# A two-layer decoder step on one core: window sums of the pooling tiles in two parts, other places for the sample's memory keys and values, and a new order of the last window groups

## The chip, the core and the metric

The kernel runs on one core of one Trainium2 chip. The metric is the device time of one launch in microseconds (us). Before the change the median of 3 runs is 1742.46 us (1741.4 to 1744.76). The profile was taken in a run of 1741.23 us, of which 1739.1 us lie between its first and its last instruction (the span).

TensorE multiplies matrices, VectorE (DVE) and ScalarE (ACT) read its results from PSUM, GpSimd (POOL) works in SBUF alone, and SyncE (SP) issues most transfers. Every engine takes its instructions in the order in which they are written; where one needs another's result, it waits on a semaphore.

## The reference, cut to what matters

One inference step: a prompt of 2048 tokens and a sample of 8 sequences of 8 tokens, width 1024, through a pooling layer (A) and a layer of sliding-window attention (B). Both share the branch that attends to 256 memory tokens with 4 heads.

```python
for i in range(N_A_LAYERS):                               # layer A
    z = rms_norm(x, norm_a[i]) @ w_in_a[i]
    u, gp, qm, gm = split(z)                              # 768, 768, 256, 256
    u_ext = concatenate([pool_prefix[i], u], axis=1)
    yp = pool_mixer(u_ext, pos, ...) * silu(gp)           # window means of 2, 4, 8, 16 rows, minus u, times mix_w
    ym = memory_branch(qm, gm, ..., mem_k[i], mem_v[i])   # softmax over 256 memory tokens
    x = x + concatenate([yp, ym]) @ w_out_a[i]
k, v = ...                                                # projected once after layer A
for j in range(N_B_LAYERS):                               # layer B
    q, gq, qm, gm = split(rms_norm(x, norm_b[j]) @ w_in_b[j])
    o = swa_banded(q, k, v, sinks)                        # prompt: blocks of 128 see themselves and the one before
    #   swa_window(q, k_all, v_all, ...)                  # sample: 128 cached keys and 8 new ones
    x = x + concatenate([o * silu(gq), memory_branch(...)]) @ w_out_b[j]
```

The prompt's memory keys and values are computed from `mem_prompt`. The sample's come from the caches `cache_mem_k` and `cache_mem_v`: per layer 8 sequences, each with 256 KB of keys and 256 KB of values in this layout.

## The kernel before

The prompt is cut into 8 tiles of 256 tokens. The program runs: a preparation (weights are scaled and split into two fp16 parts, a high and a low one), tile A0 with work of the preparation between its steps, seven more tiles of layer A, the sample in layer A (called SA), eight tiles of layer B, and the sample in layer B (SB). Every large product is three fp16 products (high x high, high x low, low x high), so a group of 256 output features for 256 tokens is 48 matmuls.

**A tile of layer A.** TensorE computes in order `qm` (memory queries), `u0` to `u2` (pooling inputs), the gates `g0` to `g2`, then `mix0` to `mix2` (the pooling products), `gm`, and four output groups `out0` to `out3`. Between them stand the memory branch's small products: transposed queries (L821), scores (L730), transposed weights (L738) and values (L748), and `largest` (L676), which spreads a maximum over all partitions for the scaling of layer B's weights; that scaling runs beside the tile on POOL (`gained`, L2300), DVE (`weight_top`, `scale_of`, `low_b`, L1621) and ACT (`high_half`, L1222). POOL normalises the queries (L2295), then waits until ACT has copied u2 and u1 (L1333), forms the running window sums of all six feature chunks together (L2374 to L2385), and normalises the softmax weights between them (`mem_norm`, L2306). DVE turns the sums into differences (L1798), and the `mix` matmuls (L768) wait for all six.

**A tile of layer B.** A window "group" is four heads of one block of 128 tokens, six groups a tile (0 to 5). Each goes round the engines: scores on TensorE (L1026), masks and maxima on DVE (`window_front`, L2094 to L2106), exponentials on ACT (L1445), sums on DVE (`window_back`), normalising on POOL (L2427), transposes on TensorE (L1034), masked weights on DVE (`window_weights`, L2124), values on TensorE (L1046), and gating on DVE (L2133). At the end of the tile the last groups alternate with pieces of the output groups (`split_out`, L778); a piece may start when DVE has split the gated features it reads (`gate_lows`, L1702).

**The sample.** Its memory keys and values come through `slot`: four places of 256 KB each. In SA the keys go through four places in `w_x` and the values through four in `x_buf`; in SB all sixteen pass through the same four places of `x_buf`. A place is loaded again when TensorE has counted up `slot_used` for the slot that it held (`load_slot`), and SP issues these loads in line with all its others. TensorE waits for each slot (`wait_slot`) in the scores (L933) and in the values (L954).

**PSUM.** `Ring` hands out banks in a fixed order: `Z` has two banks for the large products, `T` one for transposes and `largest`, `S` two for scores, `V` one for values. A writer waits until the bank's last reader is through.

```python
T = Ring(..., {"A": ["wt0", "qT", *PTM, "wt1", "ss"], ...})          # order in which T's bank is handed out
```

Of the kernel before, what the change touches and what calls it, by code (L numbers as in the profile page):

```python
# [14 lines left out]
P = 128  # L15
# [155 lines left out]
def build(nc, io):  # L171
    with ExitStack() as ctx:
# [173 lines left out]
        def slot(part, n):  # L346

            keys_a = part == "SA" and n < DB
            ring = w_x[:, 14 * P:14 * P + 2048] if keys_a else x_buf[:, 1 if part == "SA" else 0].rearrange("p k n -> p (k n)")
            return ring[:, (n % 4) * 512:(n % 4 + 1) * 512].rearrange("p (c n) -> p c n", c=2)  # L350

        def tile_of(d, t):
# [20 lines left out]
            "A": ["wt0", "qT", *PTM, "wt1", "ss"],  # L373
# [69 lines left out]
        win_sums = Signal(sem("win_sums"), {"A0": 1, "A": 1, "SA": 1})  # L443
        d_in = Signal(sem("d_in"), {"A0": 1, "A": 1, "SA": 1})
# [41 lines left out]
        def _(sp):  # L486
# [49 lines left out]
            def tile_a(t, p):  # L536
# [30 lines left out]
            for n in (*range(4, DB), *range(DB + 4, 2 * DB)):  # L567
# [28 lines left out]
            dma(io["swa_v_p"], v[:, 3]).then_inc(outputs, 16)  # L596
# [1999 lines left out]
```

## Time and profile before

| stretch | span, us | TensorE busy, us | granted clock |
|---|---|---|---|
| a tile A (344.0 to 425.0) | 81.0 | 77.04 | 1.00 |
| sample in layer A (748.5 to 812.6) | 64.1 | 40.08 | 0.76 |
| a tile B (1022.6 to 1126.7) | 104.1 | 99.40 | 1.00 |
| sample in layer B (1647.5 to 1739.1) | 91.6 | 63.99 | 0.75 |
| whole span | 1739.1 | 1574.5 | 0.967 |

The profiled execution took 1741.23 us, 2.13 us more than its span. A granted clock of 1.00 is 2.4 GHz, the higher of TensorE's two levels; a mean below 1 mixes it with 1.2 GHz. Matmuls overlap in the pipeline, so a busy TensorE isn't one at its peak, and the idle time in front of an instruction says more. In the timeline such idle time stands in brackets with what ended it; rows with "x48" merge that many instructions, from the start of the first to the end of the last.

### The profile page before, as it was taken

How to read it: one execution, taken by the hardware profiler on the slowest of the kernel's cores; microseconds unless marked ns; L12 is line 12 of the kernel's file. 1: busy time of each engine (PE TensorE's matmuls, PEld its weight loads, DVE VectorE, ACT ScalarE, POOL GpSimd, SP SyncE). 2: the span in 40 equal slices, each digit the busy share in tenths (PEclk: the TensorE clock that was granted, in tenths of full speed). 3: DMA queues.
4: the chain of work that ended last, by engine and by line, in shares of the span. 5: the costliest groups of instructions: out<-in, count | busy, mean ns of one | idle time of the engine just before them, and what ended most of it. 6: DMA issues, size and time to landing. Idle time of an engine off the chain costs nothing.

```text
span 1739.1 us, 31207 instructions
## 1 busy us (share of the span) xinstructions
PE 1574.5 (91%) x13448; PEld 1230.9 (71%) x13448; DVE 933.3 (54%) x1842; ACT 509.9 (29%) x1227; POOL 501.3 (29%) x353
## 2 busy tenths in 40 slices
PE   5787999999999999967999999999999999999976
PEld 2466888878788888855675767757586675767745
DVE  6876463545455454534563836547374563836531
ACT  2542222232323231311332514224142331514220
POOL 2631325242424142221322213132121322213120
PEclk9989999999999999987999999999999999999986
DMA  9021212122121213178101010000101001010031
GB/s 400 33 79 49 98 49 98 70 77 98 49 98 49 107 41 118 42 245 318 59 1 49 1 49 1 19 31 1 49 1 50 1 2 49 2 49 1 29 129 49
DMA packets 27400, 119.12 MB, mean 68 GB/s; under 512 B 3488, under 2 KB 3936, under 8 KB 16480
## 3 DMA queue, kind: packets, MB, share of 16 engines
q1 hardware_dynamic: 25184, 108.33, 16.7%
q10 hardware_dynamic: 2080, 8.80, 1.3%
q8 instruction: 107, 1.75, 0.4%
q14 instruction: 29, 0.24, 0.0%
HBM read 81.38 MB, written 37.64 MB: 68 GB/s over the span
## 4 chain that ended last, share of the span: by engine, by line
PE 74%; DVE 14%; ACT 5%; POOL 4%; issue 2%; DMA 1%; ACTq 0%; DVEq 0%; SPq 0%; POOLq 0%
PE ps_z L665 21%; PE ps_z L778 18%; PE ps_z L654 15%; PE ps_z L768 3%; PE ps_s L1026 2%; PE ps_z L836 2%; PE ps_t L738 2%; PE ps_p L748 2%; POOL tiny_sb L2271 2%; PE ps_p L1046 1%; DVE w_x_sb L1621 1%; DVE ph_sb L2124 1%; PE ps_z L978 1%; POOL pm_sb L2295 1%; ACT pm_sb L1258 1%
## 5 line engine op out<-in xcount | busy, mean ns | idle before, releaser
L665 PE MATMUL ps_z<-xn_sb,w_in_sb 128*128 128x256 f16 (+1 forms) x4752 | 506.6, 266 | 3.5 <-DVE gate_sb L1676 2.5
L665 PEld LDWEIGHTS ps_z<-xn_sb,w_in_sb 128*128 128x128 f16 x4752 | 429.3, 99 | 61.6 <-issue 7.1
L778 PE MATMUL ps_z<-pm_sb,w_out_sb 128*128 128x256 f16 x2048 | 348.8, 273 | 3.3 <-DVE x_buf_sb L1742 3.3
L778 PE MATMUL ps_z<-gate_sb,w_out_sb 128*128 128x256 f16 x1024 | 279.9, 273 | 0.0
L2271 POOL TENSOR_TENSOR tiny_sb<-tiny_sb 128x2 f32<-128x2 f32 (+4 forms) x56 | 94.2, 1682 | 535.7 <-DVE tiny_sb L1643 300.8
L778 PEld LDWEIGHTS ps_z<-pm_sb,w_out_sb 128*128 128x128 f16 x2048 | 202.3, 99 | 29.3 <-DVE x_buf_sb L1742 4.1
L654 PE MATMUL ps_z<-w_in_sb,xn_sb 128*128 128x512 f16 (+2 forms) x840 | 181.7, 376 | 0.0
L1634 DVE TENSOR_REDUCE tiny_sb<-scr_sb 128x8 f32<-128x512 f32 (+3 forms) x64 | 38.0, 593 | 237.4 <-ACT scr_sb L1202 157.5
L654 PEld LDWEIGHTS ps_z<-w_in_sb,xn_sb 128*128 128x128 f16 (+1 forms) x840 | 83.0, 99 | 94.1 <-issue 0.2
L1202 ACT ACTIVATE scr_sb<-ps_z,tiny_sb 128x256 f32<-128x256 f32 (+2 forms) x94 | 42.6, 489 | 346.0 <-PE ps_z L654 270.1
L778 PEld LDWEIGHTS ps_z<-gate_sb,w_out_sb 128*128 128x128 f16 x1024 | 100.5, 98 | 11.5
L1742 DVE SCALAR_TENSOR_TENSOR x_buf_sb<-ps_z,tiny_sb,x_buf_sb 128x512 f32<-128x512 f32 x64 | 48.0, 749 | 109.5 <-PE ps_z L778 109.4
L2427 POOL TENSOR_TENSOR ph_sb<-ph_sb,tiny_sb 128x512 f32<-128x512 f32 x48 | 50.0, 1042 | 193.2 <-DVE tiny_sb L2116 193.2
L1445 ACT ACTIVATE ph_sb<-ph_sb,tiny_sb 128x128 f32<-128x128 f32 x192 | 74.5, 390 | 101.5 <-DVE tiny_sb L2106 101.5
L654 PE MATMUL ps_z<-w_x_sb,xn_sb 128*128 128x512 f16 (+1 forms) x408 | 91.2, 384 | 2.3 <-issue 2.3
L2276 POOL TENSOR_TENSOR big_sb<-big_sb 128x1024 f32<-128x1024 f32 x17 | 40.0, 2354 | 170.3 <-ACT big_sb L1194 170.3
L2306 POOL TENSOR_TENSOR pm_sb<-pm_sb,tiny_sb 128x1024 f32<-128x1024 f32 x32 | 62.3, 1958 | 79.9 <-DVE tiny_sb L1669 79.9
L1216 ACT ACTIVATE xn_sb<-big_sb 128x2048 f16<-128x2048 f32 x18 | 34.4, 1911 | 167.0 <-DVE big_sb L1565 167.0
L1676 DVE SCALAR_TENSOR_TENSOR gate_sb<-scr_sb,ps_z 128x512 f32<-128x512 f32 (+1 forms) x72 | 45.9, 638 | 69.4 <-ACT scr_sb L1247 68.7
L654 PEld LDWEIGHTS ps_z<-w_x_sb,xn_sb 128*128 128x128 f16 (+1 forms) x408 | 40.5, 100 | 49.7 <-issue 4.9
L1258 ACT ACTIVATE pm_sb<-ps_s,tiny_sb 128x256 f32<-128x256 f32 x128 | 58.6, 475 | 57.6 <-DVE tiny_sb L1664 57.6
L1247 ACT ACTIVATE scr_sb<-ps_z,tiny_sb 128x512 f32<-128x512 f32 (+1 forms) x72 | 46.8, 650 | 81.9 <-PE ps_z L665 81.9
(267 smaller groups left out, 2377.8 us busy)
## 6 DMA issues: line engine op xcount, KB each, us to landing
x_buf_sb<-x SPq DMA_DIRECT2D x18, 1024.0 KB, 4.8
w_x_sb<-w_b SPq DMA_DIRECT2D x14, 1024.0 KB, 4.7
x<-x_buf_sb SPq DMA_DIRECT2D x9, 1024.0 KB, 4.0
y<-x_buf_sb SPq DMA_DIRECT2D x9, 1024.0 KB, 3.9
w_in_sb<-w_in_a SPq DMA_DIRECT2D x8, 1024.0 KB, 25.5
w_in_sb<-parts ACTq DMA_DIRECT2D x8, 1024.0 KB, 10.6
parts<-ph_sb SPq DMA_DIRECT2D x14, 512.0 KB, 3.0
parts<-w_x_sb SPq DMA_DIRECT2D x14, 512.0 KB, 3.0
```

The source lines that it names most:

```text
L654: last = mm(out, xs[:, x, kc, tok:tok + n], w[:, gs[0]:gs[-1] + 1, ws, kc, :], start=(kc == 0 and ws + x == 0), stop=(kc == KC - 1 and ws ...
L665: last = mm(ps_z[:, b, half * NT:half * NT + n], w_split[:, g, ws, kc, half * P:(half + 1) * P], xs[:, x, kc, 0:n], start=(kc == 0 and ws ...
L768: last = mm(out, mix_w[:, blocks.index((o, i)), :], src, start=(i == ins[0]), stop=(i == ins[-1]))
L778: last = mm(ps_z[:, b, half * NT:(half + 1) * NT], w_out_split[:, g, ws, kc, half * P:(half + 1) * P], gate_parts[x][:, kc, 0:NT], start=( ...
L1247: f(pair[0], pair[1], ACT.Tanh, scale=halfunit).then_inc(scr_in.sem, 1)
L1258: last = f(pm[:, blk, e, :], ps_s[:, b, e // 2, (e % 2) * NMEM:(e % 2 + 1) * NMEM], ACT.Exp, bias=m_neg[:, blk, e:e + 1], scale=SCALE, acc ...
L1445: f(sw[:, n % 2, e, :], sw[:, n % 2, e, :], ACT.Exp, bias=w_neg[:, n % 2, e:e + 1], scale=SCALE, accum_out=w_sum[:, n % 2, e:e + 1])
L1676: ve.scalar_tensor_tensor(gate[:, c:c + 2, 0:n], pair[0], 1.0, pair[1], ALU.add, ALU.mult)\
L1742: ve.scalar_tensor_tensor(x, ps_z[:, b].rearrange("p (c n) -> p c n", c=2)[:, :, 0:n], unit, x, ALU.mult, ALU.add).then_inc(Z.free[b], 1)
L2271: return tt(out, x, power[0:n, 0:w], ALU.pow)
L2306: tt(pm[:, blk], pm[:, blk], r, ALU.mult).then_inc(pm_norm.sem, 1)
L2427: tt(sw[:, i], sw[:, i], r, ALU.mult).then_inc(pw_norm.sem, 1)
```

## The change

Places, waits and order change; what is computed doesn't.

**Tiles of layer A.** POOL forms the window sums in two parts: chunks 0 to 3 as soon as u1 is copied, chunks 4 and 5 after u2. `win_sums` and `d_in` count twice a tile, DVE's `window_differences` is called twice (the first time between `silu` of g0 and g1), and `mix` waits for the first part before its first pair of chunks and for the second before its second pair. On TensorE the query transposes move from behind u2 to in front of it, `largest` into the middle of u2, the transposed weights about three quarters of a group later, and `mem_values` behind `mix`. ACT and DVE follow that order. Tile A0 keeps its order on TensorE and takes only the two parts.

**Tiles of layer B.** The last two groups stand among more and smaller pieces of output products; `silu` of g2 moves ahead of `window_back` of group 5, and its `tanh` ahead of the exponentials of group 5.

**The sample.** The slots get 13 places in SA, and in SB as many, in `w_x`, `big`, `ph` and `x_buf`. All eight keys have their own. Of the values the last four (SA) or three (SB) go where the first keys were, when `key_used` has counted those. Semaphores are per slot. Key loads are issued in the last tile in front of the sample. In SA, `square_sums` moves ahead of the first output product.

```diff
@@ slot (places)
+            if part == "SA":
+                ring, i = ((w_x[:, wx_at:wx_at + 2048], n) if n < 4 else (flat_big[:, 512:2048], n - 4) if n < 7
+                           else (ph[:, ph_at:ph_at + 512], 0) if n == 7 else (rows, n - DB) if n < DB + 4
+                           else (w_x[:, wx_at:wx_at + 2048], n - DB - 4))
+            else:
+                ring, i = ((ph[:, 0:3072], n) if n < 6 else (rows, n - 6) if n < DB
+                           else (flat_big[:, 512:2048], n - DB) if n < DB + 3 else (rows, n - DB - 1) if n < DB + 5
+                           else (ph[:, 0:3072], n - DB - 5))
@@ Ring T
-            "A": ["wt0", "qT", *PTM, "wt1", "ss"],
+            "A": ["qT", "wt0", *PTM, "wt1", "ss"],
@@ load_slot
+            last_new = DB + (4 if part == "SA" else 5)
+            if n >= last_new:
+                sp.wait_ge(key_used.sem, key_used.after(part, 0, n - last_new))
@@ sync: last tile A, SA, last tile B, SB
-                    for n in range(4):
+                    for n in (0, 1, 2, 3, 7):
+                        load_slot(sp, "SA", n, 0)
+                    sp.wait_ge(xlow_in.sem, xlow_in.after("SA", 0, -1))
+                    for n in (4, 5, 6):
                         load_slot(sp, "SA", n, 0)
...
-            for n in (*range(4, DB), *range(DB + 4, 2 * DB)):
+            for n in range(DB + 4, 2 * DB):
                 load_slot(sp, "SA", n, 0)
...
+                    if t == TILES - 1:
+                        V.wait_full(sp, "B", t, "pvw5")
+                        for n in range(6):
+                            load_slot(sp, "SB", n, 1)
...
+            sp.wait_ge(xlow_in.sem, xlow_in.after("SB", 0, -1))
+            for n in range(DB, DB + 3):
+                load_slot(sp, "SB", n, 1)
             sp.wait_ge(x_stored.sem, x_stored.after("B", TILES - 1))
-            for n in range(4):
+            for n in (6, 7, DB + 3, DB + 4):
                 load_slot(sp, "SB", n, 1)
...
-            for n in range(4, 16):
+            for n in range(DB + 5, 2 * DB):
                 load_slot(sp, "SB", n, 1)
@@ tensor: mix
-                pe.wait_ge(d_in.sem, d_in.after(part, t))
                 for pair in range(3):
+                    if pair < 2:
+                        pe.wait_ge(d_in.sem, d_in.after(part, t, pair if n == NT else 0))
@@ tensor: tile B, end
                     window_values(t, p, 3)
-                    window_transposes(t, 4)
                     pe.wait_ge(glow_in.sem, glow_in.after("B", t, 1))
                     split_out("B", t, 0, (0, 1, 6, 7), halves=(0,), first=True)
+                    window_transposes(t, 4)
+                    split_out("B", t, 0, (0, 1, 6, 7), halves=(1,), first=True)
                     window_values(t, p, 4)
+                    split_out("B", t, 1, (0, 1), halves=(0,), first=True)
                     window_transposes(t, 5)
-                    split_out("B", t, 0, (0, 1, 6, 7), halves=(1,), first=True)
+                    split_out("B", t, 1, (6, 7), halves=(0,))
+                    split_out("B", t, 1, (0, 1), halves=(1,), first=True)
                     window_values(t, p, 5)
+                    split_out("B", t, 1, (6, 7), halves=(1,))
                     pe.wait_ge(glow_in.sem, glow_in.after("B", t, 2))
                     split_out("B", t, 0, (2, 3))
-                    split_out("B", t, 1, (0, 1, 6, 7, 2, 3), first=True)
+                    split_out("B", t, 1, (2, 3))
@@ vector: window_differences
+                chunks = ((0, 1, 2, 3), (4, 5))[k]
@@ gpsimd: tile A
+                Z.wait_read(pool, part, i, "u1")
+                doubled(win_a[:, 0:4], u[:, 0:4], 2)
...
                 Z.wait_read(pool, part, i, "u2")
+                doubled(win_a[:, 4:6], u[:, 4:6], 2)
...
```

The order on TensorE in a tile of layer A before, from `u0` (the first 48 of the 96) to `mix`; `lo_sb` is `largest`, `kTm_sb` the scores, `pm_sb` the transposes, `vm_sb` the values and `w_x_sb` the `mix` matmuls:

```order
L665 MATMUL ps_z<-xn_sb,w_in_sb 128x256 x96
L676 MATMUL ps_t<-lo_sb,ones_sb 128x128
L665 MATMUL ps_z<-xn_sb,w_in_sb 128x256 x48
L821 MATMUL ps_t<-small_sb,pm_sb 128x128 x4
L730 MATMUL ps_s<-kTm_sb,ph_sb 128x256 x8
L665 MATMUL ps_z<-xn_sb,w_in_sb 128x256 x48
L738 MATMUL ps_t<-small_sb,pm_sb 128x128 x4
L665 MATMUL ps_z<-xn_sb,w_in_sb 128x256 x24
...
L748 MATMUL ps_p<-big_sb,vm_sb 64x256 x8
L768 MATMUL ps_z<-ph_sb,w_x_sb 128x256 x14
```

The same stretch of TensorE now (the line numbers are those of the changed file; L834 are the query transposes, L742 the scores, L750 the transposed weights):

```order
L677 MATMUL ps_z<-xn_sb,w_in_sb 128x256 x96
L834 MATMUL ps_t<-small_sb,pm_sb 128x128 x4
L677 MATMUL ps_z<-xn_sb,w_in_sb 128x256 x24
L688 MATMUL ps_t<-lo_sb,ones_sb 128x128
L677 MATMUL ps_z<-xn_sb,w_in_sb 128x256 x24
L742 MATMUL ps_s<-kTm_sb,ph_sb 128x256 x8
L677 MATMUL ps_z<-xn_sb,w_in_sb 128x256 x84
L750 MATMUL ps_t<-small_sb,pm_sb 128x128 x4
L677 MATMUL ps_z<-xn_sb,w_in_sb 128x256 x12
...
L781 MATMUL ps_z<-ph_sb,w_x_sb 128x256 x14
L760 MATMUL ps_p<-big_sb,vm_sb 64x256 x8
```

Between query transposes and scores there are now 48 large matmuls instead of none, and between scores and the first weight transposes 84 instead of 48.

POOL in the same tile before, from the normalised queries to the end of the window sums:

```order
L2295 TENSOR_TENSOR pm_sb<-pm_sb,tiny_sb 128x512
L2374 TENSOR_TENSOR ph_sb<-ph_sb 128x6x270
L2376 TENSOR_TENSOR ph_sb<-ph_sb 128x5x268
L2306 TENSOR_TENSOR pm_sb<-pm_sb,tiny_sb 128x1024 x2
L2380 TENSOR_TENSOR ph_sb<-ph_sb 128x3x264
L2381 TENSOR_TENSOR ph_sb<-ph_sb,ones_sb 64x256
L2383 TENSOR_TENSOR ph_sb<-ph_sb 128x2x256
L2385 TENSOR_TENSOR ph_sb<-ph_sb,ones_sb 64x256
```

POOL now (L2415 is the helper `doubled`, L2348 is `mem_norm`):

```order
L2337 TENSOR_TENSOR pm_sb<-pm_sb,tiny_sb 128x512
L2415 TENSOR_TENSOR ph_sb<-ph_sb 128x4x270
L2415 TENSOR_TENSOR ph_sb<-ph_sb 128x3x268
L2415 TENSOR_TENSOR ph_sb<-ph_sb 128x264
L2427 TENSOR_TENSOR ph_sb<-ph_sb,ones_sb 64x256
L2415 TENSOR_TENSOR ph_sb<-ph_sb 128x2x270
L2415 TENSOR_TENSOR ph_sb<-ph_sb 128x2x268
L2348 TENSOR_TENSOR pm_sb<-pm_sb,tiny_sb 128x1024 x2
L2415 TENSOR_TENSOR ph_sb<-ph_sb 128x2x264
L2415 TENSOR_TENSOR ph_sb<-ph_sb 128x2x256
L2440 TENSOR_TENSOR ph_sb<-ph_sb,ones_sb 64x256
```

The same 4264 elements a partition go through in seven sums instead of four, and four instructions of them stand ahead of the wait for u2.

DVE at the end of a tile of layer B before, from the masked weights of group 4 (the first L2124) to those of group 5; L2114 and L2116 are `window_back` of group 5, L1676 is `silu` of g2, L1702 a gate split, L2133 gating:

```order
L2124 TENSOR_TENSOR ph_sb<-ps_t,small_sb 128x512 x2
L2114 TENSOR_TENSOR tiny_sb<-tiny_sb 128x4
L2116 RECIPROCAL tiny_sb<-tiny_sb 128x4
L1676 SCALAR_TENSOR_TENSOR gate_sb<-scr_sb,ps_z 128x512
L1702 TENSOR_TENSOR gate_sb<-gate_sb,pm_sb 128x2x256
L2133 SCALAR_TENSOR_TENSOR gate_sb<-ps_p,tiny_sb,gate_sb 128x2x128
L2124 TENSOR_TENSOR ph_sb<-ps_t,small_sb 128x512 x2
```

The same stretch of DVE now (L2166 are the masked weights, L1714 is `silu`, L2156 and L2158 are `window_back`, L2175 gating, L1740 a gate split):

```order
L2166 TENSOR_TENSOR ph_sb<-ps_t,small_sb 128x512 x2
L1714 SCALAR_TENSOR_TENSOR gate_sb<-scr_sb,ps_z 128x512
L2156 TENSOR_TENSOR tiny_sb<-tiny_sb 128x4
L2158 RECIPROCAL tiny_sb<-tiny_sb 128x4
L2175 SCALAR_TENSOR_TENSOR gate_sb<-ps_p,tiny_sb,gate_sb 128x2x128
L1740 TENSOR_TENSOR gate_sb<-gate_sb,pm_sb 128x2x256
L2166 TENSOR_TENSOR ph_sb<-ps_t,small_sb 128x512 x2
```

`silu` of g2 now stands in front of `window_back` of group 5, which POOL waits for, and the gating of group 4 in front of the gate split.

## Rows read from the trace of the kernel before

**Rows 1.** Stretches: length; busy (instructions) of PE, PEld, DVE, ACT, POOL; clock; DMA.
```profile
344.00:425.00 81.00, 77.04 (x672) 67.57 (x670) 41.70 (x63) 22.62 (x39) 29.71 (x18) 1.00 0.21 79
...
748.50:812.60 64.10, 40.08 (x664) 33.66 (x665) 21.73 (x58) 11.18 (x25) 15.28 (x26) 0.76 0.73 277
...
1022.60:1126.70 104.10, 99.40 (x822) 72.59 (x820) 59.05 (x130) 32.48 (x101) 28.35 (x21) 1.00 0.06 21
```

**Rows 2.** Waits of PE, whole span: line waited for, total us, times, longest.
```profile
PE ps_p L1046 <- DVE ph_sb L2124: 17.1, 24, 1.4
PE ps_t L1034 <- POOL ph_sb L2427: 13.9, 16, 1.1
PE ps_s L730 <- ACT ph_sb L1252: 13.7, 8, 1.9
...
PE ps_t L738 <- POOL pm_sb L2306: 8.5, 5, 1.7
```

**Rows 3.** Timeline of PE, a tile A: start, us, instruction, [idle before].
```profile
359.81 5.40 PE L665 MATMUL ps_z<-xn_sb,w_in_sb 128*128 128x256 f16 x48
...
367.51 2.00 PE L730 MATMUL ps_s<-kTm_sb,ph_sb 64*128 64x256 f32 x16 [1.86 <-ACT ph_sb L1252]
...
376.56 0.66 PE L738 MATMUL ps_t<-small_sb,pm_sb 128*128 128x128 f32 x4 [1.70 <-POOL pm_sb L2306]
```

**Rows 4.** Timeline of POOL, the same tile A.
```profile
366.02 2.89 POOL L2374 TENSOR_TENSOR ph_sb<-ph_sb 128x1620 f32<-128x1620 f32 x1 [11.51 <-ACT ph_sb L1333]
368.98 3.28 POOL L2376 TENSOR_TENSOR ph_sb<-ph_sb 128x1340 f32<-128x1340 f32 x1
374.61 3.75 POOL L2306 TENSOR_TENSOR pm_sb<-pm_sb,tiny_sb 128x1024 f32<-128x1024 f32 x2 [2.34 <-DVE tiny_sb L1669]
```

**Rows 5.** Timeline of DVE, the same tile A.
```profile
371.15 1.14 DVE L1664 TENSOR_SCALAR tiny_sb<-tiny_sb 128x4 f32<-128x4 f32 x1
...
373.45 0.17 DVE L1664 TENSOR_SCALAR tiny_sb<-tiny_sb 128x4 f32<-128x4 f32 x1
```

**Rows 6.** Timeline of PE, end of a tile B.
```profile
1098.97 0.63 PE L1034 MATMUL ps_t<-small_sb,ph_sb 128*128 128x128 f32 x4 [1.10 <-POOL ph_sb L2427]
...
1102.33 1.09 PE L1046 MATMUL ps_p<-ph_sb 128*64 128x128 f32 x16 [1.42 <-DVE ph_sb L2124]
1104.06 0.66 PE L1034 MATMUL ps_t<-small_sb,ph_sb 128*128 128x128 f32 x4 [0.63 <-POOL ph_sb L2427]
...
1106.53 1.09 PE L1046 MATMUL ps_p<-ph_sb 128*64 128x128 f32 x16 [0.51 <-DVE ph_sb L2124]
```

**Rows 7.** Timeline of DVE, the same end of a tile B.
```profile
1103.60 0.69 DVE L1676 SCALAR_TENSOR_TENSOR gate_sb<-scr_sb,ps_z 128x512 f32<-128x512 f32 x1 [0.72 <-ACT scr_sb L1247]
```

**Rows 8.** Timeline of PE, sample in layer A.
```profile
763.21 3.87 PE L933 MATMUL ps_s<-w_x_sb,ph_sb 128*32 128x256 f32 x16 [5.17 <-DMA w_x_sb<-mem_ks]
...
775.60 0.44 PE L945 MATMUL ps_t<-small_sb,pm_sb 128*128 128x128 f32 x2 [1.60 <-issue]
...
777.42 1.09 PE L954 MATMUL ps_p<-x_buf_sb,big_sb 128*32 128x256 f32 x16 [0.47 <-ACT big_sb L1252]
782.62 3.98 PE L954 MATMUL ps_p<-x_buf_sb,big_sb 128*32 128x256 f32 x16 [4.11 <-DMA x_buf_sb<-mem_vs]
```

**Rows 9.** Timeline of POOL, sample in layer A: its window sums.
```profile
756.18 6.79 POOL L2415 TENSOR_TENSOR ph_sb<-ph_sb 128x176 f32<-128x176 f32 x16 [1.55 <-ACT ph_sb L1415]
```

**Rows 10.** Timeline of PE, sample in layer B.
```profile
1686.84 4.31 PE L933 MATMUL ps_s<-x_buf_sb,w_in_sb 128*32 128x256 f32 x16 [2.66 <-DMA x_buf_sb<-mem_ks]
1691.57 0.55 PE L1164 MATMUL ps_t<-small_sb,w_in_sb 96*128 96x96 f32 x4 [0.42 <-POOL w_in_sb L2451]
1694.36 0.90 PE L1164 MATMUL ps_t<-small_sb,w_in_sb 96*128 96x96 f32 x4 [2.23 <-DVE w_in_sb L2247]
...
1709.66 1.96 PE L954 MATMUL ps_p<-x_buf_sb,big_sb 128*32 128x256 f32 x16 [0.47 <-ACT big_sb L1252]
1714.16 4.34 PE L954 MATMUL ps_p<-x_buf_sb,big_sb 128*32 128x256 f32 x16 [2.54 <-DMA x_buf_sb<-mem_vs]
```

More of the change, by code:

```diff
@@ L853, in tile_a @@
                 else:
+                    q_transposes_a(part, i)
+                split_features(part, i, "u2", 3, halves=(0,))
+                if not start:
                     largest(part, i, 0, "wt0")
-                split_features(part, i, "u2", 3)
+                split_features(part, i, "u2", 3, halves=(1,))
                 if start:
@@ L858, in tile_a @@
                     memory_keys(1)
-                q_transposes_a(part, i)
-                T.wait_read(pe, part, i, "qT")
+                    q_transposes_a(part, i)
+                T.wait_read(pe, part, i, "qT" if start else "wt0")
                 mem_scores(part, i, 0, qT_a, 0)
@@ L883, in tile_a @@
                     mix_sums("l1a", range(0, 4))
-                mem_values(part, i)
+                    mem_values(part, i)
+                else:
+                    mem_transposes(part, i, 1, 1)
                 if start:
@@ L890, in tile_a @@
                 mix(part, i, NT)
+                if not start:
+                    mem_values(part, i)
                 if start:
@@ L1788, in _, with window_differences @@
             ve.memset(u[:, :, 0:16], 0.0).then_inc(u_free.sem, 1)
-            def window_differences(part, i):
-                dve.wait_ge(win_sums.sem, win_sums.after(part, i))
+            def window_differences(part, i, k):
+                dve.wait_ge(win_sums.sem, win_sums.after(part, i, k))
+                chunks = ((0, 1, 2, 3), (4, 5))[k]
                 if part == "A0":
-                    own(ve.tensor_tensor(win_a[:, 0:4:3, 16:32], win_a[:, 0:4:3, 16:32], corr[:, 0:4:3, :], ALU.mult))
-                    own(ve.tensor_tensor(win_b[:, 1:6, 16:32], win_b[:, 1:6, 16:32], corr[:, 1:6, :], ALU.mult))
+                    for c in chunks:
+                        own(ve.tensor_tensor(pooled(c)[:, 16:32], pooled(c)[:, 16:32], corr[:, c, :], ALU.mult))
                     own.wait()
-                for c in range(POOLC):
+                for c in chunks:
                     last = ve.scalar_tensor_tensor(pooled(c)[:, 16:UW], pooled(c)[:, 16:UW], invw[:, c:c + 1],
@@ L1901, in tile_a @@
                     low_b(part, i, 0, 0)
-                    low_b(part, i, 0, 1)
                 for blk in range(NBLK):
                     mem_max(part, i, blk)
+                if not begin:
+                    low_b(part, i, 0, 1)
                 if begin:
@@ L1917, in tile_a @@
                     weight_top("A0", 0, 2, "stage_b")
+                window_differences(part, i, 0)
                 silu(part, i, "g1", 2, 2)
@@ L1921, in tile_a @@
                     mix_top(0, "l1a", 4)
-                window_differences(part, i)
+                window_differences(part, i, 1)
                 if begin:
```

109 lines of the change are left out of this document (61 added, 48 removed).

## The prediction

> **What bounds the kernel now.** I read the busy times by stretch first, then TensorE's waits over the whole span, then the timelines of the stretches that the diff touches. In the stretches [rows 1] TensorE is busy for 77.04 of a tile A's 81.0 us and for 99.40 of a tile B's 104.1, at a granted clock of 1.00 (2.4 GHz); no other engine comes to 68 us in either. In the sample in layer A it is busy for 40.08 of 64.1 us, at a mean clock of 0.76, and the transfers run at a share of 0.73. So TensorE sets the end everywhere, the number of its large products doesn't change, and a gain can only be idle time in front of its instructions. The waits [rows 2] name that time: scores for the query copy (13.7 us in 8 waits), weight transposes for POOL's `mem_norm` (8.5 in 5), and in layer B the window groups: values for DVE (17.1 in 24), transposes for POOL (13.9 in 16). The sample's waits are read where they stand [rows 8, 10].
>
> **Tiles A (7 with the new order).** One large matmul takes 5.40 / 48 = 0.1125 us [rows 3]. Two waits of TensorE stand in the tile [rows 3]: 1.86 us in front of the scores and 1.70 in front of the weight transposes, 3.56 together.
>
> - Scores: the query transposes move ahead of u2, so that 48 matmuls (5.4 us) lie where none did. The transposes' copy was 1.86 us late; it is then about 3.5 early. What is late next is `largest`'s reader, since the scores' bank order now lets them follow `scale_of` on DVE: only 24 matmuls (2.7 us) lie between. DVE's small operations can be held up by POOL: L1664 takes 0.17 us alone, and 1.14, ending when POOL's second sum ends, beside it [rows 4, 5]. POOL's first part can start when u1 is copied: the sums before began 0.81 us after u2's end (366.02 against 359.81 + 5.40), so now about 360.6. Its 1080, 804 and 264 elements cost 1.8 to 2.45 ns each (2.89 / 1620 and 3.28 / 1340 [rows 4]), 4.3 us at the mean of these, and with the 64-partition sum about 5.1: to 365.7, while the scores are due at 365.65 (367.51 less 1.86). A `scale_of` held to the very end costs some 0.2 us; I charge 0.16.
> - Weight transposes: 84 matmuls now lie between the scores and them instead of 48, so they are due 36 x 0.1125 = 4.05 us later, plus 1.86 earlier scores the other way. Against `mem_norm` the margin goes from -1.70 to about +0.5 or more, since the softmax starts earlier too, and one sum part is out of POOL's way. Gain 1.70.
> - POOL: the same 4264 elements in seven sums instead of four, three instructions more. They lie in the 11.51 us that POOL waited for the copies [rows 4]; `mix` waits for the second part, which is shorter than the whole was. Without that cover each extra sum costs at most its fixed part, some 0.1 to 0.5 us by the difference of the two rates above. DVE's `window_differences` in two calls, and `mem_values` behind `mix`, lie beside products of 5.4 us each. I cost them at nothing.
>
> Sum: 3.56 - 0.16 = 3.4 a tile, 7 x 3.4 = 23.8 us. Bounds: only the first wait goes and a little returns, 2.0 a tile (14); all of it, 3.56 (25). Tile A0 keeps its order; 0, give or take 0.5.
>
> The rule of the Trainium skill that speaks against this is in "SBUF — State Buffer", section "Who interferes with whom": VectorE and GpSimd share one pair of ports, whoever takes it keeps it for its whole instruction, and the other stops. The 1.14 against 0.17 us agrees with it. By the rule more and earlier POOL sums mean more DVE instructions held up; what that would cost is the first rival.
>
> **Sample in layer A.** Keys: TensorE had its first four slots scored at 763.21 - 5.17 = 758.04, then stood for the transfers, and ended the last four at 763.21 + 3.87 = 767.08 [rows 8]: 9.04 us, where four slots that are there take 1.09 (the first values, at 777.42). The keys now have their own places and are issued in the tile before: 9.04 - 1.09 = 7.95. What is late next: POOL's window sums end at 756.18 + 6.79 = 762.97 [rows 9], and the softmax then needs POOL once more, at most the 3.75 / 2 = 1.9 us of one instruction of L2306 in a tile [rows 4], so to 764.9; the weight transposes would be due no sooner than now less 7.95, 775.60 - 7.95 = 767.65. Not binding. Values: from 777.42 to 782.62 + 3.98 = 786.60, 9.18 us; with all slots there 2 x 1.09 = 2.18, a gain of 7.0. `square_sums` ahead of the first output product is the same work elsewhere, 0. Sum 14.95, taken as 15. Bounds: the transfers already have a share of 0.73, and the weights that follow the slots on SP's queue (it takes its loads in line) now start earlier too, so some of the wait can come back at the next weight: 5 at the low end (one of the two waits, less a third). High end 17: the 1.60 in front of the weight transposes goes too.
>
> **Tiles B (8).** Four waits [rows 6]: transposes of group 4 for POOL 1.10, values for DVE 1.42, transposes of group 5 0.63, values 0.51: 3.66. DVE's order up to the weights of group 4 is the same, so the values of group 4 can go no sooner than about 1102.3: the 1.1 + 1.42 ahead of them are filled by the half piece of output that now stands between, and what remains is about 1.4. `silu` of g2, 0.69 us [rows 7], now stands in front of `window_back` of group 5, which POOL waits for, and after POOL TensorE: the transposes of group 5 come about 0.4 late. The values of group 5 aren't late any more. Three more pieces of six matmuls lie in front of them, 18 x 0.1125 = 2.0 us, and this is the work that filled the holes; the waits left are 1.4 + 0.2 of 3.66, a gain of 2.1 (3.66 less 1.6), which agrees with those 2.0. 8 x 2.1 = 16.8. Bounds: 0 if DVE's chain moves along, 3.66 x 8 = 29 if every wait goes. The last gate split follows the groups; the rows don't show its margin, and what it may cost lies within the low bound.
>
> **Sample in layer B.** The key wait of 2.66 us is in front of L933 [rows 10]; it ends at 1691.15, and 0.42 us later the next work waits for POOL's window chain (L2451), which doesn't depend on the keys. So most of it turns into that wait; only part of the 2.23 behind it (DVE's multiplication, no longer behind the memory's reciprocal) can go: 1.2. Values: from 1709.66 to 1714.16 + 4.34 = 1718.50, 8.84 us, against 2 x 1.96 = 3.92, a gain of 4.9. Sum 6.1, taken as 6; bounds 3 (values alone, and late ones) to 7.
>
> **Sum.** 23.8 + 15 + 16.8 + 6 = 61.6. The profiled run took 1741.23 us (span 1739.1 and 2.13 around it): 1679.6. The median of the runs shown is 1.23 above that run, so about 1681.
>
> **Rivals.**
> 1. POOL's earlier sums hold DVE up in the tiles A. For it: L1664 at 1.14 beside POOL [rows 5], and the first part runs just when `scale_of` is due. Against: `scale_of`'s operations are few, and TensorE has 2.7 us. If two operations on the way to the scores are held by 1.14 - 0.17 = 0.97 us each, the gain is 3.4 - 1.94 = 1.5 a tile, 7 x 1.5 = 10.5 instead of 23.8: 1694. Chance 0.12.
> 2. The transfers in the sample in layer A are still the limit: share 0.73 [rows 1], the same bytes. For it: places free earlier don't make bytes move faster. Against: the keys start a tile earlier, when the share is 0.21 [rows 1]. Gain 5 instead of 15: 1691. Chance 0.12.
> 3. The clock in the samples rises as the waits go. TensorE's rows there show a mean of 0.76 for 40.08 us [rows 1]; at 1.00 these would take 40.08 x 0.24 = 9.6 less; half of it is 5: 1676. Against: the waits of the long small-operation chains remain. Chance 0.10.
> 4. In the tiles B DVE's chain moves with the pieces, so that the same 3.66 us stand elsewhere: 16.8 go, 1698. For it: the values of group 4 wait for the same DVE work. Chance 0.08.
> 5. Slower: the fuller tiles lose the full clock. 7 tiles A of 77.5 and 8 tiles B of 102 are 1358 us at 1.00; the gain of 61.6 is eaten when the mean clock there falls to 1358 / (1358 + 61.6) = 0.957. At 0.95 it costs 71.5: 1751. Against: the clock is 1.00 where TensorE is 95% busy, and lower only where it waits [rows 1]. Chance 0.02.
>
> The Trainium skill, "TensorE: Matmul & The Clock Gate", section "What's actually happening", says that the throttled state is the default and that activity releases it. The rows agree (1.00 in the tiles, 0.76 in the sample); by it rival 3 is favoured over rival 5.
>
> **How the numbers follow.** The forecast, 1681, has 0.56. The cases from 1676 to 1698 are within 17 us of it. For the range I add the terms' low ends not all at once: half of the shortfalls (10 in A, 10 in the sample, 17 in B, 3 in SB: 40) is 20, so 1699 would be high; at the other end 1 + 2 + 12 + 1 = 16 of further gain, of which 13: 1668. The range 1668 to 1699 leaves out less than 2 in 10. What a measurement of this kernel can tell from no change is about 0.2%, 3.5 us. Faster by more than that: 0.97; within it 0.01 (only if two rivals meet); slower 0.02.
>
> **What would show it.** A tile A's period down from 81 to about 77.5, with no wait of TensorE in front of scores and weight transposes; a wait of scores for `scale_of` would point to rival 1. A tile B's period near 102, with the wait of 1.4 us for DVE at the values of group 4 left, and no longer waits in front of group 5. No wait for a transfer at L933 and L954 of either sample; if one stands at the output weights instead, rival 2. The granted clock in the samples tells of rival 3, in the tiles of rival 5. The prediction is wrong if the tiles' periods stay as they are, or if the last gate split or the second part of the window sums takes the place of the waits that go.

## The result and the profile after

The changed kernel takes 1681.82 us in the median (1681.34 to 1682.75, 4 runs), the kernel before 1742.62 (1741.4 to 1744.76, 4 runs): a ratio of 0.965 (95% interval 0.9634 to 0.9667), 60.8 us less. The forecast was 1681. The time agrees to a microsecond, but terms of the sum were wrong in opposite directions: 8 us too much in the sample in layer A, 7 too little in the tiles A and in A0.

To see where the time went, I cut both profiles at one instruction that every tile has, DVE's scaling of the next tile's x (`big_sb<-x_buf_sb`, L1565 before, L1603 after), and took the distances between its starts:

| stretch | before, us | after, us | gained | forecast |
|---|---|---|---|---|
| start to the end of tile A0 | 171.37 | 167.98 | 3.4 | 0 |
| seven tiles A (80.89 to 76.96 each; the first 82.17 to 78.22) | 567.53 | 539.96 | 27.6 | 23.8 |
| sample in layer A | 67.06 | 60.03 | 7.0 | 15 |
| first tile B | 104.82 | 103.80 | 1.0 | 2.1 |
| seven tiles B (104.14 to 102.03) | 728.98 | 714.22 | 14.8 | 14.7 |
| sample in layer B | 99.34 | 93.51 | 5.8 | 6 |
| span | 1739.1 | 1679.5 | 59.6 | 61.6 |

The stretches of the changed kernel that answer to [rows 1] (columns as there):

```profile
332.60:409.56 76.96, 76.56 (x671) 67.40 (x669) 44.64 (x62) 22.85 (x39) 29.23 (x21) 1.00 0.23 83
717.50:774.60 57.10, 39.83 (x665) 32.63 (x665) 21.07 (x58) 10.96 (x25) 14.81 (x26) 0.78 0.83 318
981.50:1083.50 102.00, 99.48 (x823) 72.52 (x821) 59.75 (x130) 32.60 (x101) 28.40 (x21) 1.00 0.06 22
```

In a tile A TensorE is now busy for 76.56 of 76.96 us; there is nothing left to cover. In the sample in layer A it still idles for 17 us, and the transfers' share rose from 0.73 to 0.83. TensorE's waits over the whole span, which answer to [rows 2] (L1070 is the window values, L980 the sample's values):

```profile
PE ps_p L1070 <- DVE ph_sb L2166: 12.0, 16, 1.3
...
PE ps_p L980 <- DMA w_x_sb<-mem_vs: 5.3, 3, 3.0
...
PE ps_s L742 <- ACT ph_sb L1280: 0.7, 1, 0.7
```

The waits for the query copy (13.7 us), for POOL's window norm (13.9) and for `mem_norm` (8.5) are gone, but for one of 0.7 in tile A0; the window values wait 12.0 us instead of 17.1. TensorE in a tile A, answering to [rows 3], has no wait at the query transposes (L834), the scores (L742) or the weight transposes (L750):

```profile
348.31 0.60 PE L834 MATMUL ps_t<-small_sb,pm_sb 128*128 128x128 f32 x4
348.75 2.78 PE L677 MATMUL ps_z<-xn_sb,w_in_sb 128*128 128x256 f16 x24
...
354.31 2.00 PE L742 MATMUL ps_s<-kTm_sb,ph_sb 64*128 64x256 f32 x16
...
365.42 0.60 PE L750 MATMUL ps_t<-small_sb,pm_sb 128*128 128x128 f32 x4
```

POOL in the same tile, answering to [rows 4] (L2348 is `mem_norm`):

```profile
349.28 4.30 POOL L2415 TENSOR_TENSOR ph_sb<-ph_sb 128x1080 f32<-128x1080 f32 x3 [6.04 <-ACT ph_sb L1361]
...
360.48 3.75 POOL L2348 TENSOR_TENSOR pm_sb<-pm_sb,tiny_sb 128x1024 f32<-128x1024 f32 x2 [2.71 <-DVE tiny_sb L1707]
```

`mem_norm` of the first block ends about 362.4 (the row merges two of equal size), 3 us ahead of the transposes. The end of a tile B, answering to [rows 6]: of four waits one is left, 1.26 us for DVE at the values of group 4.

```profile
1058.05 0.60 PE L1058 MATMUL ps_t<-small_sb,ph_sb 128*128 128x128 f32 x4
...
1061.22 1.09 PE L1070 MATMUL ps_p<-ph_sb 128*64 128x128 f32 x16 [1.26 <-DVE ph_sb L2166]
...
1063.22 0.66 PE L1058 MATMUL ps_t<-small_sb,ph_sb 128*128 128x128 f32 x4
...
1065.26 1.09 PE L1070 MATMUL ps_p<-ph_sb 128*64 128x128 f32 x16
```

The sample in layer A on TensorE, answering to [rows 8]: keys without a wait for a transfer (L959), but three such waits among the last four slots of values (L980, four matmuls a slot), and matmuls at half speed behind them (a slot 1.92 us instead of 1.05, the mix products 6.24 instead of 3.34 before; from 749.1 to 755.4 the granted clock is 0.50).

```profile
725.98 1.09 PE L959 MATMUL ps_s<-w_x_sb,ph_sb 128*32 128x256 f32 x16 [1.13 <-ACT ph_sb L1316]
...
735.38 0.41 PE L971 MATMUL ps_t<-small_sb,pm_sb 128*128 128x128 f32 x2
...
737.18 1.09 PE L980 MATMUL ps_p<-x_buf_sb,big_sb 128*32 128x256 f32 x16 [0.47 <-ACT big_sb L1280]
...
740.13 1.05 PE L980 MATMUL ps_p<-w_x_sb,big_sb 128*32 128x256 f32 x4 [1.03 <-DMA w_x_sb<-mem_vs]
744.22 1.92 PE L980 MATMUL ps_p<-w_x_sb,big_sb 128*32 128x256 f32 x4 [3.04 <-DMA w_x_sb<-mem_vs]
747.32 1.92 PE L980 MATMUL ps_p<-w_x_sb,big_sb 128*32 128x256 f32 x4 [1.19 <-DMA w_x_sb<-mem_vs]
749.16 6.24 PE L781 MATMUL ps_z<-ph_sb,w_x_sb 128*128 128x64 f32 x28
```

And why, as e1 and e3 below show: SP issues those four loads (1 MB) at 729.29, and ACT issues four weight loads of 1 MB each from 729.50 on. SP's row, then ACT's:

```profile
729.29 2.27 SPq L478 DMA_DIRECT2D w_x_sb<-mem_vs  x4
```

```profile
729.50 0.33 ACTq L1467 DMA_DIRECT2D w_in_sb<-parts  x1
...
730.36 1.42 ACTq L1467 DMA_DIRECT2D w_in_sb<-parts  x2
```

In the kernel before, the two lay 10 us apart, ACT's first; ACT's row, then SP's:

```profile
768.21 0.33 ACTq L1429 DMA_DIRECT2D w_in_sb<-parts  x1
```

```profile
778.50 2.87 SPq L473 DMA_DIRECT2D x_buf_sb<-mem_vs  x4
```

The sample in layer B, answering to [rows 10]:

```profile
1629.40 1.30 PE L959 MATMUL ps_s<-ph_sb,w_in_sb 128*32 128x256 f32 x18 [0.36 <-DVE w_in_sb L2258]
...
1637.89 0.90 PE L1192 MATMUL ps_t<-small_sb,w_in_sb 96*128 96x96 f32 x4 [6.51 <-POOL w_in_sb L2506]
1640.13 0.90 PE L1192 MATMUL ps_t<-small_sb,w_in_sb 96*128 96x96 f32 x4 [1.34 <-DVE w_in_sb L2289]
...
1659.85 1.11 PE L990 MATMUL ps_t<-small_sb,pm_sb 128*128 128x128 f32 x4 [0.74 <-ACT pm_sb L1310]
```

### The profile page after: what moved, and what is told of

Same layout as the page of the kernel before. It is cut to its first block, busy times and chain, and to the rows that moved or that the text cites. A ratio compares the mean times of both kernels' runs of the same rounds, so it can differ in the third digit from the quotient of the medians.

```text
span 1679.5 us, 31237 instructions
## 1 busy us (share of the span) xinstructions
PE 1560.9 (93%) x13448; PEld 1223.0 (73%) x13448; DVE 956.4 (57%) x1846; ACT 511.9 (30%) x1227; POOL 506.6 (30%) x377
## 4 chain that ended last, share of the span: by engine, by line
PE 77%; DVE 13%; POOL 4%; ACT 2%; DMA 2%; issue 2%; SPq 0%; DVEq 0%; POOLq 0%; ACTq 0%
PE ps_z L677 23%; PE ps_z L791 18%; PE ps_z L666 16%; PE ps_z L781 3%; PE ps_s L1050 2%; PE ps_z L849 2%; PE ps_p L760 2%; DVE ph_sb L2166 2%; PE ps_t L750 2%; POOL tiny_sb L2313 2%; PE ps_p L1070 1%; PE ps_s L742 1%; POOL pm_sb L2337 1%; PE ps_t L1058 1%; DMA w_x_sb<-mem_vs 1%
## 5 line engine op out<-in xcount | busy, mean ns | idle before, releaser
L2415 POOL TENSOR_TENSOR ph_sb<-ph_sb 128x1080 f32<-128x1080 f32 (+6 forms) x56 | 75.0, 1340 | 70.5 <-ACT ph_sb L1361 67.9
L2348 POOL TENSOR_TENSOR pm_sb<-pm_sb,tiny_sb 128x1024 f32<-128x1024 f32 x32 | 62.3, 1958 | 77.9 <-DVE tiny_sb L1707 77.9
L1280 ACT ACTIVATE big_sb<-ps_t 128x512 f32<-128x512 f32 (+1 forms) x68 | 39.5, 581 | 98.2 <-PE ps_t L750 82.0
```

The costliest lines, as they stand in the source:

```text
L2348: tt(pm[:, blk], pm[:, blk], r, ALU.mult).then_inc(pm_norm.sem, 1)
L2415: own(tt(out[..., at:UW], src[..., at:UW], src[..., at // 2:UW - at // 2], ALU.add))
```

## The experiments

Each is timed against the kernel before on the same chip (medians of four runs; the three marked "one run" ran once). The kernel before took 1740.1 to 1742.6 us beside them. In the next three, a, b and s stand for the parts of the diff on tiles A, on tiles B and on the sample. Stretches are read from one profile of each kernel.

**The three parts alone.** The kernel before with one part of the diff each, here in words:

```diff
 a_only: + win_sums/d_in twice, two-part sums, Ring T "qT","wt0", TensorE/ACT/DVE order of tile A
 b_only: + split_out pieces, silu/tanh of g2 and window_back earlier
 s_only: + slot places, key_used, loads, square_sums
```

> The kernel before with the tile-A part of the change alone (two-part window sums, new order). Theory (each removed wait gives back its idle time and the 0.16 us of drain of the four matmuls ahead of it): a tile A's period 76.96 instead of 80.89, 7 x 3.93 = 27.5 us less, 1715.1 us. Rival (the 3.4 us by which the changed kernel's first tile ends earlier also belong to this part, since it is the only part that touches that tile): 31 us less, 1711.7, and the first tile's end at 168.0 in the profile instead of 171.4. If only the idle time counts: 7 x 3.56 = 24.9, 1717.7.

Measured: 1712.06 us, ratio 0.9833 (0.9816 to 0.985); tiles A of 76.96, the end of A0 at 167.33.

> The kernel before with the tile-B part alone (smaller output pieces between the last groups, silu of g2 and tanh earlier). Theory: period 102.03 instead of 104.14, 8 x 2.11 = 16.9 us less, 1725.7 us; the wait of about 1.26 us for DVE at the values of group 4 stays. Rival (part of the gain comes from the other parts' clock or timing): less than 14 us.

Measured: 1723.64 us, ratio 0.9902 (0.9884 to 0.9921); tiles B of 102.01, tiles A of 80.90.

> The kernel before with the sample part alone (places, loads, square_sums). Theory: in the sample in layer A 9.3 us gained before the values, 2.9 lost at the values and 2.1 at the mix products (half clock), some 2.7 gained after them, 1.1 lost in the first tile of layer B; 5.8 gained in the sample in layer B; together 11 to 12 us, 1731. Rival (the loss at the values comes from the fuller tile A in front, not from this part): 15 + 6 = 21 us, 1722.

Measured: 1727.54 us, ratio 0.9921 (0.9903 to 0.994); the sample in layer A 58.92 us against 67.06, the one in layer B 94.18 against 99.34, tiles as before.

What follows: the three gains make 30.5 + 19.0 + 15.1 = 64.6 us, against 60.8 together; each of these differences of medians is uncertain by some 3 us, so this doesn't show the parts to help or hinder each other. The loss at the sample's values is no matter of the fuller tiles in front: with its own part alone the sample in layer A gains 8.1, not 15, and has the same three waits for the last values (1.11, 2.10 and 2.04 us). And tile A0 belongs to part A: with it A0 ends 119.7 to 121.2 us behind the first cut in every profile but one (below), without it 122.3 to 123.0.

**Loads of the weights later (e1).** ACT's first four loads go behind its copies of the transposed weights.

```diff
-            for g in range(4):
-                nc.scalar.dma_start(w_split[:, g], io["parts"][g])...
             for i, g in enumerate((*G3, "gm")): tanh("SA", ...)
             sample_weights("SA")
+            for g in range(4):
+                nc.scalar.dma_start(w_split[:, g], io["parts"][g])...
```

> The changed kernel with ACT's first four weight loads (4 MB) in the sample in layer A issued behind its copies of the transposed weights instead of ahead of the tanh. Theory 1 (the last four values, 1 MB, share the transfer engines with those 4 MB, issued 0.2 us later): no waits in front of the values, 5.3 us and the half clock behind them (2.9 us in the mix products) come back: 8 to 10 us less, 1672 to 1674. Theory 2 (they are late because SP issues them at 729.3, behind the store of x and the keys' places): the waits stay, 1681 to 1683. Theory 3 (the weights then come late for the first tile of layer B): the waits go and a wait for w_in stands in that tile, 1676 or more.

Measured: 1674.76 us (1674.13 to 1675.15), ratio 0.9618 (0.9601 to 0.9636), against 0.965 of the changed kernel: 7.1 us less. The values wait for no transfer, and the clock stays at 1.00 through the mix products. TensorE in that kernel:

```profile
736.27 1.09 PE L980 MATMUL ps_p<-x_buf_sb,big_sb 128*32 128x256 f32 x16 [0.47 <-ACT big_sb L1280]
737.15 1.12 PE L980 MATMUL ps_p<-w_x_sb,big_sb 128*32 128x256 f32 x16
738.21 3.34 PE L781 MATMUL ps_z<-ph_sb,w_x_sb 128*128 128x64 f32 x28
...
754.97 1.01 PE L644 MATMUL ps_t<-ones_sb,big_sb 128*128 128x1 f32 x4 [10.38 <-POOL big_sb L2322]
```

SP issued the same loads at the same point (729.11), so the store and the places ahead of them aren't the cause; theory 1 holds. The median from issue to landing fell from 12.1 to 6.3 us. From the start of the values to the end of the mix products the kernel is quicker by 12.9 us (18.2 to 5.3), but some 6.8 are lost again behind them, where TensorE now waits 10.38 us for POOL: the 4 MB now go out together with the next tile's x, whose load took 9.8 us instead of 4.8 and whose squares POOL sums. That this is the cause is what e3 tries.

**Loads behind that x too (e3), and with `square_sums` back (e2, e4).**

```diff
 e3:  squares_x("SA", 0, 0, 1, 16 * 6)
+     for g in range(4): nc.scalar.dma_start(w_split[:, g], io["parts"][g])...   # moved from ahead of tanh
 e2 (alone), e4 (with e3):
-     square_sums(T, "SA", 0, "ss", 0)
      sample_out("SA", 0)
+     square_sums(T, "SA", 0, "ss", 0)
```

> The changed kernel with ACT's first four weight loads (4 MB) issued behind the squares of the next tile's x, instead of ahead of the tanh. With those loads behind the transposed weights only, x landed 9.8 us after its issue, and TensorE waited 10.4 us for POOL's sums of its squares. Theory (x shares the transfer engines with the 4 MB as the values did): x lands about 4.9 us earlier, 1669.8. Rival (x is slow by itself, or the weights now come late for the first tile of layer B): 1675 or more, with a wait for w_in in that tile in the second case.

Measured: 1670.41 us (1670.18 to 1671.81), ratio 0.9595 (0.958 to 0.9611). x lands after 4.7 us, the wait for POOL is 5.40, and the first tile of layer B takes 102.48 us, with no wait for a transfer of its weights. The sample in layer A now takes 48.98 us, 18.1 less than before the change. ACT's row and its loads:

```profile
742.98 1.91 ACT L1222 ACTIVATE big_sb<-x_buf_sb 128x2048 f32<-128x2048 f32 x1 [4.11 <-DMA x_buf_sb<-x]
742.99 1.86 ACTq L1472 DMA_DIRECT2D w_in_sb<-parts  x4
```

> The changed kernel with square_sums behind the first output product again. The prediction's step (0): 1681.8, the stretch from the last mix product to the first tile of layer B as it is. Theory (in front of the output product it fills the wait for DVE's gate split, and the chain to the next tile, square_sums, rstd, diagonals, starts earlier): about 2.2 us more, 1684.

Measured: 1681.74 us (1679.97 to 1683.32): no difference to 1681.82. In the profile the sample takes 1.76 us more and the first tile of layer B 1.10 less (its first 48 matmuls 12.21 us instead of 13.29). So the two nearly cancel, the 2.2 us were not there, and the prediction's 0 for this step stands in the total.

> As the run before, with square_sums behind the first output product again. Theory (the wait for POOL's sums is still some 5 us, and the output product, 4.2 us, fits into it): about 2 us less than the run before, 1668. Rival (the order square_sums first is better in either case, by the 2 us expected of the run that undoes it in the changed kernel): 1672.

Measured: 1669.88 us (1669.16 to 1672.18), the same as e3 within the scatter; the theory (1668) and the rival (1672) aren't told apart. Either version beats both kernels: 11 to 12 us under the changed one, 70 to 71 under the one before.

**Sums undivided (e5, one run).** POOL's sums, DVE's differences and the wait of `mix` as before, in all tiles A (and so no early start either); the new order stays.

```diff
-    doubled(win_a[:, 0:4], u[:, 0:4], 2) ... doubled(win_a[:, 4:6], u[:, 4:6], 2) ...
+    tt(win_a[:, 0:6, 2:UW], u[:, :, 2:UW], u[:, :, 1:UW - 1], ALU.add) ...
-    window_differences(part, i, 0); window_differences(part, i, 1)
+    window_differences(part, i)
```

> The changed kernel with the window sums undivided in all tiles A, on POOL, DVE and in the wait of mix; the new order of TensorE, ACT and DVE stays. Theory (the split pays at mix, which is due 19.4 us after the end of u2 instead of 25.6): POOL's sums end about 369.5 in the tile that has mix due at 373.7, six differences of 1.2 us end about 376.8, so a wait of 3 to 5 us in front of mix and a period of 80 to 82 us; no wait at the weight transposes. Rival A (the split is what lets mem_norm in time): a wait of 1 to 2 us at the weight transposes. Rival B (the order alone makes the gain): 76.96.

Measured: 1699.81 us. The five tiles A in which POOL also scales a weight take 79.33 to 81.02 us (the first 82.29, against 78.22 in the changed kernel), the last two 76.96. The wait stands at `mix`, and in three of the five the clock falls behind it (28 matmuls take 7.97 us there, at a mean clock of 0.78 to 0.79, and 6.28 in the other two, at 1.00, behind the same wait; a tile with 7.97):

```profile
385.53 7.97 PE L780 MATMUL ps_z<-ph_sb,w_x_sb 128*128 128x256 f32 x28 [2.14 <-issue]
```

DVE's six differences end at 385.43 there (379.64 + 5.79), 0.1 us ahead of it. So the theory's place is right and its wait of 3 to 5 us was 2.14. They take 5.79 us beside POOL's scaling of a weight; in the sixth of the seven tiles, without that scaling, they take 2.46 and are done 1.1 us before `mix` starts:

```profile
379.64 5.79 DVE L1835 SCALAR_TENSOR_TENSOR ph_sb<-ph_sb,small_sb 128x256 f32<-128x256 f32 x6 [1.36 <-POOL ph_sb L2423]
...
621.01 2.46 DVE L1835 SCALAR_TENSOR_TENSOR ph_sb<-ph_sb,small_sb 128x256 f32<-128x256 f32 x6 [1.35 <-POOL ph_sb L2423]
```

Nothing waits at the weight transposes. In this kernel A0 took 122.96 us again, so A0's gain comes from the division, too.

**First part only after u2 (e7, one run).**

```diff
-                if begin:
-                    Z.wait_read(pool, part, i, "u2")
+                Z.wait_read(pool, part, i, "u2")
                 Z.wait_read(pool, part, i, "u1")
```

> The changed kernel with POOL's first window part held back until u2 is copied (two parts, two differences as in the changed kernel, only the early start is gone), in all tiles A. Theory (the division, not the early start, is what mix needs: first differences ready some 10 us ahead of mix, the second part about when its pair of chunks is due): 76.96 with at most 0.5 more in the tiles where POOL also scales a weight. Rival (POOL's sums then push mem_norm back: it would end at 364.6 for the first block in the tile whose transposes are due at 365.4, 366.5 for the second): a wait of up to 1 us at the weight transposes or at mix, 77.5 to 79.

Measured: 1685.43 us; tiles of 77.45, the last two of 77.38. A wait of 0.20 us stands at the first weight transposes of each: the rival's place, the theory's size. Against e5, the division alone (without the early start) is worth 1.9 to 3.6 us in five tiles; the early start of the divided sums 0.4 to 0.5 in all seven.

```profile
366.24 0.66 PE L750 MATMUL ps_t<-small_sb,pm_sb 128*128 128x128 f32 x4 [0.20 <-POOL pm_sb L2348]
```

**DVE and ACT in the tiles B as before (e6, one run).**

```diff
-                    window_back(t, 4); gate_lows("B", t, 1, 6)
+                    gate_lows("B", t, 1, 6); window_back(t, 4)
-                    silu("B", t, "g2", 9, 4); window_back(t, 5); window_gated(t, 4); gate_lows("B", t, 2, 2)
+                    window_back(t, 5); silu("B", t, "g2", 9, 4); gate_lows("B", t, 2, 2); window_gated(t, 4)
 ACT:
-                    window_exps(t, 4); tanh("B", t, "g2", ...); window_exps(t, 5)
+                    window_exps(t, 4); window_exps(t, 5); ...; tanh("B", t, "g2", ...)
```

> The changed kernel with DVE's and ACT's order in the tiles B as it was (window_back of group 4 behind the gate split, silu of g2 and its tanh late); TensorE keeps the new order with its smaller pieces. The prediction's step (DVE's order ahead of the weights of group 4 unchanged, the pieces fill the holes): a period of 102.0 to 102.3. Theory (window_back of group 4, which now stands ahead of a gate split of some 0.7 us, took 1.1 us of the wait for POOL with it, and the gate split behind silu of g2 releases the next piece): 102.7 to 103.5, with a longer wait at the values of group 4 or a wait of output pieces for the gate split. Rival: 104.1, the order alone makes the gain.

Measured: 1689.94 us. A tile B takes 102.64, 0.62 more; one takes 104.20 and the first 105.85, for which I have no cause. TensorE waits 0.92 us at the second output group for DVE's `silu` of g2 (L1714), not longer at the values of group 4. By the order of `Z` that output group takes the PSUM bank that g2 was in, so `silu` has to have read it:

```profile
961.77 1.09 PE L1070 MATMUL ps_p<-ph_sb 128*64 128x128 f32 x16 [1.30 <-DVE ph_sb L2166]
963.78 0.28 PE L791 MATMUL ps_z<-pm_sb,w_out_sb 128*128 128x256 f16 x1 [0.92 <-DVE gate_sb L1714]
```

So of 2.11 us a tile the smaller pieces make 1.5, and DVE's and ACT's order 0.6. My theory had the place wrong.

## Why the prediction came out right, step by step

**Tiles A: right in mechanism, 0.53 us a tile too small.** Both waits went. The 0.16 that I charged for `scale_of` wasn't needed: it ends at 353.1, 1.2 us ahead of the scores. The rest is a wait that costs more than its idle time. Two rows of before, beside those of [rows 3]:

```profile
365.05 0.60 PE L821 MATMUL ps_t<-small_sb,pm_sb 128*128 128x128 f32 x4
...
369.44 5.41 PE L665 MATMUL ps_z<-xn_sb,w_in_sb 128*128 128x256 f16 x48
```

The transposes began at 365.05 and the scores behind them at 367.51, 2.46 us; now 0.44 us lie between the transposes and the next matmuls (348.31 to 348.75). That is a gain of 2.02 where the row says 1.86: without a wait the next matmul starts 0.16 us before the row of the transposes (0.60) ends, and a wait loses that overlap. The other wait gave 1.88 for its 1.70 in the same way.

POOL's first part started with u1's copy and took 4.30 us, where I had 4.3. There my working was loose: 2148 elements at the mean of the two rates are 4.5, and the higher rate is no pace of the sums, for the same sum of 1340 elements takes 2.42 us (1.8 ns an element) in A0 below, and 3.28 in [rows 4]. The fixed part of a sum doesn't follow from these two rates either.

**The cost of the division: right at nothing, its worth not seen.** I costed two parts at nothing and asked only what they delay. e5 shows what they carry: `mix` is due 19.4 us after u2 instead of 25.6, since the two waits (2.02 and 1.88), the query transposes (0.44) and `mem_values` (1.88) no longer lie between. Undivided sums miss it by 2.14 us in the five tiles in which POOL also scales a weight, and not in the last two.

**Tile A0: wrong (0, give or take 0.5; measured about 2).** A sum of all six chunks held DVE up, and shorter sums do so less. POOL's second sum and beside it DVE's low part of a weight of layer A (`low`), in A0 without part A (b_only), POOL's row first:

```profile
102.76 2.42 POOL L2380 TENSOR_TENSOR ph_sb<-ph_sb 128x1340 f32<-128x1340 f32 x1
```

and DVE's:

```profile
103.66 3.67 DVE L1625 SCALAR_TENSOR_TENSOR w_in_sb<-x_buf_sb,tiny_sb,w_in_sb 128x2048 f16<-128x2048 f32 x1 [0.95 <-ACT w_in_sb L1226]
```

With part A (a_only) the same DVE instruction takes 2.57 us, and the one that is held is POOL's short sum over 64 partitions, 2.53 us where it takes 0.61 in b_only. DVE's row, then POOL's:

```profile
103.81 2.57 DVE L1645 SCALAR_TENSOR_TENSOR w_in_sb<-x_buf_sb,tiny_sb,w_in_sb 128x2048 f16<-128x2048 f32 x1 [1.86 <-ACT w_in_sb L1236]
```

```profile
104.31 2.53 POOL L2413 TENSOR_TENSOR ph_sb<-ph_sb,ones_sb 64x256 f32<-64x256 f32 x1
```

A wait of 0.80 us at `largest` goes, and 24 matmuls behind a later wait take 2.78 instead of 4.43 us (granted clock 1.00 instead of 0.61). All profiles agree: in the four kernels with undivided sums the DVE instruction takes 3.66 to 3.67 us and the 24 matmuls 4.08 to 4.45, in the eight with divided sums 2.57 to 2.58 and 2.78. Why the clock falls in the one case and not in the other, no run shows. The first rival had this mechanism with the wrong sign: it asked where more POOL sums would hold DVE, and not where shorter ones free it. In the tiles A DVE is held as well (a 128x4 operation 0.96 us beside a sum, [rows 5] has 0.17 alone), but nothing waits for it. The rest of the 3.4 us lies ahead of the first cut, at 48.33 us in the profile of before and at 46.71 to 48.08 in all others.

**Sample in layer A: the step that failed.** "with all slots there 2 x 1.09 = 2.18, a gain of 7.0": of the last four values three were not there. From the first value to the last took 12.06 us (737.18 to 747.32 + 1.92), before 9.18, a loss of 2.9, and the mix products another 2.9 at half the clock. The keys' step held: from the start to the weight transposes 17.9 us instead of 27.1, 9.2 gained, the 7.95 and most of the 1.60. Behind the mix products 3.5 more are gained (16.1 to 12.6 us up to the next cut; 1.8 of them by `square_sums`, by e2), which with the two losses makes the 7.0 measured. But the keys' gain is what moved the failure. ACT's 4 MB wait for the score softmax, so without the key wait they go out 12.0 us after the sample's start instead of 19.8; and SP's last values, which waited for a place until 30.1 us after it, now take the first keys' places and go out at 11.8. Rival 2 came nearest (the same bytes, at a limit), with 5 us instead of 15; I looked for it at the output weights, and it stood at the values. But the bytes as such were no limit: e1 and e3 move the same bytes later, the values then take 1.9 to 2.0 us, near the 2.18 of the sum, and in e3 the sample gains 18.1 us. What failed was the order in which the loads go out. The clock's part has its place in rival 3, reversed: over the sample its mean is 0.78 where it was 0.76, and behind the new waits it fell, from 1.00 before 738 to 0.59 until 762.6. The page that I quoted there, the Trainium skill's "TensorE: Matmul & The Clock Gate", section "What's actually happening", has it that activity releases the throttle. These rows agree, and in e1 and e3, where no such wait stands ahead of them, the same 28 matmuls take 3.34 us.

**Tiles B: right, 2.11 against 2.1.** The wait left is 1.26 where I had 1.4. Its reason was half right: I wrote that DVE's order ahead of the weights of group 4 doesn't change, but `window_back` of group 4 did move ahead of a gate split, and e6 shows that the new order on DVE and ACT carries 0.6 of it, at an output piece that waits for `silu` of g2. The first tile gained 1.1 less than the others, by a slower clock at its start (13.29 us for its first 48 matmuls at 0.79, 12.21 at 0.86 before); with `square_sums` back (e2) they take 12.21 again.

**Sample in layer B: right in sum (5.8 against 6), its parts shifted.** The keys gave nothing at all: 8.49 us from the first key scores to the window transposes, before 8.48; the wait for keys became one of 6.51 for POOL. The second transposes gave 0.55 (2.24 us after the first, against 2.79), the values 5.1 (4.41 us up to the next transposes, against 9.52).

So the total is right by luck: 8 us too much in one sample met 7 us too little in the tiles A and A0. The tiles and the sample in layer B came as forecast, the sample in layer A nearer to rival 2. The range held too, though its ends were counted from two starts (1699 is 20 above 1679.6, 1668 is 13 below 1681).

## What to carry to other kernels

When a wait goes, the loads that were queued behind it go out earlier too, on every queue: before counting a load as "there", list every load that another queue will issue in the same microseconds, with its bytes. Move the loads that are needed last behind those that are needed first, on whichever queue they are (here 11 us for moving three lines). And when a step is moved earlier, check what its inputs' producers now have in hand: the division of the sums was costed as an expense, and is what keeps `mix` from waiting in five of seven tiles.

## What the runs showed that I had not expected

- In a tile A a wait costs its idle time and some 0.16 us of lost overlap: 1.86 idle gave 2.02, 1.70 gave 1.88 (from the start of the 48 matmuls ahead of it to the transposes 7.12 us, where 48 matmuls without a wait take 5.24). In a tile B it isn't so: the four waits went from 3.66 to 1.26, 2.40 less, and 2.11 came back.
- Behind the same wait of 2.14 us the clock fell in three of e5's tiles and not in two: 28 matmuls took 7.97 or 6.28 us (81.02 or 79.33 us a tile). What decides it, no run shows.
- A load's time from issue to landing doubled beside 4 MB of others: the last values 12.1 us instead of 6.3, x 9.8 instead of 4.8.
